# One core of a hybrid SSD and HGRN2 layer: HGRN's tile products grouped into seven visits, raised block by block

## The chip, the cores and the metric

The kernel runs on one core of one Trainium2 chip, and is written engine by engine: each engine's instructions stand in the order of the code and wait on semaphores. TensorE multiplies, VectorE, ScalarE and GpSimd work elementwise, SyncE issues most of the transfers. The metric is the device time of one execution in microseconds (us); lower is better.

## The reference

One inference step of a layer over 1,152 tokens (128 of context, 1,024 latent): a combined input projection feeds two mixers, a Mamba-2 SSD and an HGRN2, whose outputs are gated, merged and followed by a feed-forward block. What the change touches is HGRN2's scan, forward and backward, for each of 8 heads:

```python
c = HGRN_CHUNK
b = jnp.cumsum(log_f.astype(f32).reshape(bt, nc, c, n_heads, kd), axis=2)
causal = jnp.tril(jnp.ones((c, c), dtype=bool))[:, :, None, None]
decay = jnp.exp(jnp.where(causal, b[:, :, :, None] - b[:, :, None, :], -jnp.inf))
attn = jnp.einsum("bcihk,bcijhk,bcjhk->bcijh", qc, decay, kc)
o_intra = jnp.einsum("bcijh,bcjhv->bcihv", attn, vc)
contrib = jnp.einsum("bcjhk,bcjhv->bchkv", kc * jnp.exp(b[:, :, -1:] - b), vc)
...
o = o_f + o_b[:, ::-1]
```

The kernel takes chunks of 128 tokens. It builds `attn` of a chunk by levels: at level lv, blocks of 2^(lv-1) tokens meet their neighbours, with keys and queries that carry the decay up to the block's edge; between levels keys and queries are multiplied by the neighbour's decay ("raised").

## The kernel before

The token axis is cut into three blocks of 384 (`NB` = 3, `BW` = 384), a block into three chunks of 128 (`CB`). After a prologue the mixers run over 8 groups (`g`), one HGRN head and four SSD heads each. A group has two halves of 18 slots. In every slot TensorE projects one unit (a weight tile against one block): 24 matmuls of 384 columns into one of two banks that alternate, so that slot k needs the bank that slot k-2 filled to be free (`bank_free`). In the second half (`stage_b`) the slots 3 to 14 belong to convolution tiles; their unit is taken out of its bank in this order, in each slot k:

- ScalarE: `conv_tanh(k-1)`, which waits until VectorE has ended the taps of slot k-1; then `b_evac(k)`, a scaled copy of the bank to `acc`.
- VectorE: `conv_silu(k-1)` (th times acc, both in SBUF), which waits for that tanh; then `b_evac(k)`, four taps from the bank onto `acc`; the last one frees the bank. In slots 5, 8, 11 and 14 (block 0, context and latent) they are eight instructions. Once in three slots `low` subtracts a weight tile (`w_lo`).

Between these stands HGRN's work of the same group. TensorE makes the products of levels 0 to 7, three blocks each, 24 steps in all; a step is 12 matmuls of 32x32 tiles (levels 0 to 6) or 6 of 64x64 (level 7). Two steps follow the unit of each of the slots 0 to 11 (`steps_in`); such a stop between projection matmuls is called a visit here. Level lv from 1 to 5 needs a copy of the block's keys, ScalarE's `ka` (two buffers, `ka[i % 2]`, one of them a part of `kt_all`), levels 6 and 7 read `kq` itself. GpSimd raises a block with two multiplications of `kq` once TensorE has made its product (`lv_ready`), and tells by `up_ready`; ScalarE's copy for the next level waits for that. GpSimd walks the steps slot by slot too. VectorE collects a level's result when its third block is there (COPY_PREDICATED into `at_in`, one level a time; after level 5 four copies to `at_all`), and joins the decays of neighbouring blocks for the next levels (`join_decays`, at the slots of `JOINS`: 2, 4, 5, 6), in slots up to 4 ahead of silu and taps, in slots 5 and 6 behind them. The joins of slot 5 are two multiplications, those of slot 6 three. In slots 12 to 16 TensorE turns keys, sums states and makes the outputs. In the last group, g = 7, the second half has 24 units of gate columns instead; ScalarE alone empties their banks, and VectorE has no taps.

Nothing here is scheduled by a compiler: the order is the code's.

Of the kernel before, what the change touches and what calls it, by code (L numbers as in the profile page):

```python
# [540 lines left out]
def mixers(nc, scope, sb, sem, m):  # L541
# [75 lines left out]
    with ExitStack() as hgrn_scope:  # L617
# [82 lines left out]
    hrstd_ok, o_final, o_stored, soh_stored = sem("hrstd_ok"), sem("o_final"), sem("o_stored"), sem("soh_stored")  # L700

# [43 lines left out]
    with nc.Block() as block:  # L745
# [128 lines left out]
        def _(pe):  # L874
            def project(g, t, b, hb, cols_n=P):
# [120 lines left out]

            def hgrn(g, k):
                for i in steps_in(k):
                    lv, b = level(i)
                    if lv == 0:  # L1000
                        pe.wait_ge(q_ready, g * 3 + 1)
# [4 lines left out]
                    if b == 0:  # L1006
                        if lv == 1 or lv == 4:
                            pe.wait_ge(ms_read, g * NB + (2 if lv == 1 else 3))
                        elif lv == 3 or lv == 5:
                            pe.wait_ge(v_kept, g * NB + (2 if lv == 3 else 3))  # L1010
                        elif lv > IN_BLOCK:
                            pe.wait_ge(lv_merged.sem, lv_merged.at(g, 1 if lv == 6 else 5))
                    for j in range(CB):
                        c = b * CB + j
                        s = 1 << (lv - 1) if lv else 0
                        w = max(BS, s)
                        for t in range(P // w):
                            rows = slice(w * t, w * (t + 1))
                            out = lv_out(lv, b)[rows, j * w:(j + 1) * w]
                            own = slice(c * P + w * t, c * P + w * (t + 1))  # L1020
                            other = slice(c * P + w * (t ^ 1), c * P + w * ((t ^ 1) + 1))
                            if lv == 0:
                                last = pe.matmul(out, k_sum[:, own], q_t[:, own], start=True, stop=True)
                            elif lv <= IN_BLOCK:
                                last = pe.matmul(out.rearrange("p (n two s) -> p n two s", two=2, s=s),  # L1025
                                                 ka[i % 2][:, j * P + w * t:j * P + w * (t + 1)],
                                                 pairs(1, 2, s, c * P + w * t, w), start=True, stop=True)
# [122 lines left out]
            for k in range(8 * NB):  # L1150
                project(g, 6 + k // NB, k % NB, k % NB)
# [6 lines left out]
        def _(act):  # L1158
# [142 lines left out]

            def hgrn(g, k):
# [6 lines left out]
                for i in steps_in(k):  # L1309
                    lv, b = level(i)  # L1310
                    if lv == 0 or lv > IN_BLOCK:
                        continue
                    if lv == 1:
                        act.wait_ge(q_ready, g * 3 + 3)
                    else:
# [3 lines left out]
                    act.activation(ka[i % 2][:, :].rearrange("p (n two s) -> p n two s", two=2, s=s),  # L1319
                                   pairs(0, 3, s, b * BW, BW), ACT.Copy).then_inc(ka_ready.sem, 1)  # L1320
# [130 lines left out]
            def stage_b(g):  # L1451
                for k in range(SLOTS):
# [5 lines left out]
                    if k == 12:  # L1458
                        load_states(g)
# [1968 lines left out]
```

## Time and profile before

| | us |
|---|---|
| median of 3 runs | 3008.42 (3008.14 to 3009.68) |
| the profiled execution | 3008.66 |
| its span, first to last instruction | 3006.8 |
| TensorE busy in it | 2974.6 (99%) |
| VectorE, ScalarE, GpSimd busy | 1750.1, 1351.9, 941.0 |

The profiled execution lies 0.24 us over the median, and 1.9 us of it lie outside the span. The granted TensorE clock was 0.998 of full speed. A busy share of TensorE counts pipelined matmuls by modelled ends; how fast it goes is read from the distance between starts. Below, times inside the span are those of the group g = 2, whose second half begins at about 687 us; the other groups before g = 7 show the same pattern 202.25 us apart.

### The profile page before, as it was taken

What the parts mean: (1) busy time and instruction counts of PE and PEld (TensorE: products, weight loads), DVE (VectorE), ACT (ScalarE), POOL (GpSimd) and SP (SyncE); (2) the same over time, 40 slices, a digit from 0 to 9 for tenths busy, and PEclk for the clock granted to TensorE, in tenths of its full rate; (3) what the DMA queues carried; (4) which work ended last, traced back from release to release, by engine and by line L of the source; (5) the groups of instructions that cost most, each with busy time, mean ns of one, the idle gap of its engine ahead of it and who ended that gap; (6) DMA issues with size and microseconds to landing.
All of it is one profiled execution on the core that took longest, in us unless ns stands there. A gap on an engine that the chain in (4) does not pass through costs nothing. (4 is left out here: it accounts for less than half of the span.)

```text
span 3006.8 us, 57473 instructions
## 1 busy us (share of the span) xinstructions
PE 2974.6 (99%) x22229; PEld 2827.9 (94%) x22229; DVE 1750.1 (58%) x3007; ACT 1351.9 (45%) x2651; POOL 941.0 (31%) x1086
## 2 busy tenths in 40 slices
PE   7999999999999999999999999999999999999999
PEld 5899999999999999999999999999999999998887
DVE  4746857668577476585684624344378445555554
ACT  6445456455554554555645543211253222234443
POOL 0024435246245353462453430000113343340110
PEclk9999999999999999999999999999999999999999
DMA  7723122122122131221222325442312322227552
GB/s 266 260 69 102 49 79 81 48 78 81 47 89 73 59 99 43 83 81 49 74 80 67 118 80 161 141 124 86 122 40 61 87 65 76 76 65 248 201 184 103
DMA packets 294016, 300.29 MB, mean 100 GB/s; under 512 B 13240, under 2 KB 254768, under 8 KB 293808
## 3 DMA queue, kind: packets, MB, share of 16 engines
q1 hardware_dynamic: 247968, 230.17, 24.5%
q10 hardware_dynamic: 45840, 67.27, 7.1%
q8 instruction: 141, 2.31, 0.3%
q14 instruction: 67, 0.55, 0.1%
HBM read 247.93 MB, written 49.46 MB: 99 GB/s over the span
## 5 line engine op out<-in xcount | busy, mean ns | idle before, releaser
L889 PE MATMUL bank<-h_hi,w_hi 128*128 128x384 f32 x2496 | 863.4, 346 | 0.0
L889 PE MATMUL bank<-h_hi,w_lo 128*128 128x384 f32 x2496 | 835.7, 335 | 0.0
L889 PE MATMUL bank<-h_lo,w_hi 128*128 128x384 f32 x2496 | 834.9, 335 | 0.0
L889 PEld LDWEIGHTS bank<-h_hi,w_hi 128*128 128x128 f32 x2496 | 468.9, 188 | 12.7 <-issue 7.3
L889 PEld LDWEIGHTS bank<-h_lo,w_hi 128*128 128x128 f32 x2496 | 469.4, 188 | 0.6
L889 PEld LDWEIGHTS bank<-h_hi,w_lo 128*128 128x128 f32 x2496 | 468.6, 188 | 0.0
L2033 POOL TENSOR_TENSOR kq<-kq,fg 128x384 f32<-128x384 f32 x288 | 291.1, 1040 | 161.4 <-PE bank L1025 130.5
L1562 DVE SCALAR_TENSOR_TENSOR acc<-bank,taps,acc 128x372 f32<-128x372 f32 (+5 forms) x512 | 249.1, 507 | 68.0 <-ACT acc L1189 56.6
L1277 ACT ACTIVATE cumb<-cumb,tok_g 128x128 f32<-128x128 f32 x576 | 176.0, 389 | 75.5 <-POOL cumb L1994 75.5
L2440 PE MATMUL bank<-a_hi,v_hi 128*128 128x384 f32 x480 | 160.9, 335 | 2.9 <-DVEq L3238 1.9
L1530 DVE TENSOR_TENSOR w_lo<-raw,w_hi 128x1024 fp32r<-128x1024 f32 x104 | 140.4, 1350 | 38.3 <-ACT w_hi L1170 38.3
L2440 PE MATMUL bank<-a_hi,v_lo 128*128 128x384 f32 x480 | 160.4, 334 | 0.0
L2440 PE MATMUL bank<-a_lo,v_hi 128*128 128x384 f32 x480 | 160.4, 334 | 0.0
L2478 PE MATMUL bank<-a_hi,v_lo 128*128 128x288 f32 x480 | 141.6, 295 | 0.0
L2478 PE MATMUL bank<-a_hi,v_hi 128*128 128x288 f32 x480 | 141.2, 294 | 0.1
L2478 PE MATMUL bank<-a_lo,v_hi 128*128 128x288 f32 x480 | 141.3, 294 | 0.0
L1941 POOL TENSOR_TENSOR tok_g<-tok 128x36 f32<-128x36 f32 x16 | 4.2, 261 | 403.8 <-DVE q_t L1769 300.4
L1176 ACT ACTIVATE th<-acc 128x384 f32<-128x384 f32 x96 | 50.4, 525 | 173.6 <-DVE acc L1562 173.6
L1994 POOL TENSOR_SCALAR_AFFINE_SELECT cumb<-cumb 128x512 f32<-128x512 f32 x144 | 96.3, 691 | 83.5 <-DMA cumb<-cum_scratch 83.5
L1958 POOL TENSOR_TENSOR xp<-xb,tok_g 128x256 f32<-128x256 f32 x128 | 83.2, 657 | 114.5 <-PE bank L925 95.2
L3318 POOL MEMSET small<- 128x384 f32 x3 | 1.1, 418 | 373.7 <-issue 373.7
L2440 PE MATMUL bank<-b_hi,v_hi 128*128 128x384 f32 x336 | 113.0, 336 | 0.4 <-DVE b_lo L3225 0.2
(389 smaller groups left out, 6891.8 us busy)
## 6 DMA issues: line engine op xcount, KB each, us to landing
raw<-in_w_in SPq DMA_DIRECT2D x104, 512.0 KB, 4.0
raw<-in_ffn_w SPq DMA_DIRECT2D x78, 512.0 KB, 5.7
cumb<-cum_scratch SPq DMA_DIRECT2D x72, 512.0 KB, 6.1
ada_late<-in_ada_w SPq DMA_DIRECT2D x8, 2048.0 KB, 9.2
raw_d<-in_ffn_w SPq DMA_DIRECT2D x32, 512.0 KB, 5.3
small<-gate_scratch ACTq DMA_DIRECT2D x72, 192.0 KB, 2.4
hid_scratch<-small SPq DMA_DIRECT2D x20, 576.0 KB, 3.6
s_sum<-hid_scratch ACTq DMA_DIRECT2D x53, 192.0 KB, 3.6
```

The costliest lines, as they stand in the source:

```text
L889: last = pe.matmul(out, w[i][:, k, :], h[:, k, blk(hb)], start=(k == 0 and j == 0), stop=(k == KT - 1 and j == 2))
L1176: act.activation(th[ui][:, :], acc[ui][:, :], ACT.Tanh).then_inc(th_ok.sem, 1)
L1277: last = act.activation(e, e, ACT.Exp, bias=tok_g[:, 0, c, r:r + 1])
L1530: dve.tensor_tensor(w_lo[i][:, :, 0:width], raw[i][:, :, 0:width], w_hi[i][:, :, 0:width].bitcast(F32), ALU.subtract).then_inc(w_split.sem, 1)
L1562: ins = dve.scalar_tensor_tensor(out, src, taps[:, ti, j:j + 1], out, ALU.mult, ALU.add)
L1941: pool.tensor_tensor(dst[0], of_group(tok[:, 0, :, :], d), of_group(tok[:, 2, :, :], d), ALU.subtract)
L1958: return pool.tensor_tensor(out.rearrange("p (h c) -> p h c", c=HD), x.rearrange("p (h c) -> p h c", c=HD), w.rearrange("p (h a) -> p h a" ...
L1994: ins = pool.affine_select(v, v, [[0, HPG], [sign, P]], ALU.is_ge, far, base=0, channel_multiplier=-sign)
L2033: ins = pool.tensor_tensor(v, v, w.broadcast_to([P, 2, n, s]), ALU.mult)
L2440: last = pe.matmul(banks[3 * s + b][:, 0:BW], w[wp][:, k, :], operand[ap][:, k, blk(b)], start=(k == 0 and j == 0), stop=(k == kt - 1 and ...
L2478: last = pe.matmul(out, w[wi][:, k, :], mv, start=(o < 4 and k == 0 and i == 0), stop=(k == KH - 1 and i == 2), skip_group_check=o >= 4)
L3318: pool.memset(tmp[b][:, :], 0.0).then_inc(sums_zero, 1)
```

## The change

The two steps a slot are gone. A table `BURSTS` gives seven places, counted in eighths of a unit (three projection matmuls) from the half's start: levels 0 and 1 after slot 1's unit (16), level 2 in slot 3 (31), 3 in slot 5 (44), 4 in slot 7 (57), 5 in slot 8 (70), 6 in slot 10 (82), 7 in slot 11 (92); each place takes all three blocks. `project` stops inside a unit where the table says so. `ka` has a third buffer, a part of `hs_f`, so that each block has its own. GpSimd runs through `UPS`, all 21 raises, waiting for product, decay and the raise below, no longer slot by slot; level 7 goes in the order 0, 2, 1. ScalarE's copies stand in a table, most at a slot's start, two behind its tanh (`KA_LATE`). VectorE collects the levels in the slots of `MERGES`, and the joins of slot 5 move ahead of its silu and taps.

```diff
+BURSTS = {16: (0, 1), 31: (2,), 44: (3,), 57: (4,), 70: (5,), 82: (6,), 92: (7,)}
+KA_EARLY = {1: [(1, 0), (1, 1), (1, 2)], 2: [(2, 0)], 3: [(2, 1), (2, 2)], 4: [(3, 0), (3, 1)], 5: [(3, 2)],
+            6: [(4, 1), (4, 2)], 7: [(5, 0)], 8: [(5, 2)]}
+KA_LATE = {5: [(4, 0)], 7: [(5, 1)]}
+UPS = [(lv, b) for lv in range(1, LEVELS + 1) for b in ((0, 2, 1) if lv == LEVELS else range(NB))]
+MERGES = {2: (0, 1), 4: (2,), 5: (3,), 7: (4,), 9: (5,)}
+KEEPS = {10: [(6, 2)], 12: [(7, 1), (7, 2)]}
...
+        ka.append(hs_f[:, 3:6, :].rearrange("p c n -> p (c n)"))
...
+    up_ready = Count(sem("up_ready"), len(UPS))
...
+    def raised(eng, g, lv, b):
+
+        eng.wait_ge(up_ready.sem, up_ready.at(g, UPS.index((lv, b)) + 1))
...
-            def project(g, t, b, hb, cols_n=P):
+            def project(g, t, b, hb, cols_n=P, between=None):
...
                 for k in range(KT):
+                    if between is not None and k > 0:
+                        levels_at(g, KT * between + k)
                     for j, (w, h) in enumerate(((w_hi, h_hi), (w_hi, h_lo), (w_lo, h_hi))):
...
+            def levels_at(g, at):
+
+                for lv in BURSTS.get(at, ()):
+                    for b in range(NB):
+                        level_step(g, lv, b)
+
+            def level_step(g, lv, b):
+                i = step(lv, b)
+                if lv == 0:
+                    pe.wait_ge(q_ready, g * 3 + 1)
+                elif lv <= IN_BLOCK:
+                    pe.wait_ge(ka_ready.sem, ka_ready.at(g, i - NB + 1))
+                else:
+                    raised(pe, g, lv - 1, b)
+                if b == 0:
...
+                                             ka[b][:, j * P + w * t:j * P + w * (t + 1)],
...
             def hgrn(g, k):
-                for i in steps_in(k):
-                    lv, b = level(i)
...
-                    elif lv <= IN_BLOCK:
-                        pe.wait_ge(ka_ready.sem, ka_ready.at(g, i - NB + 1))
-                    else:
-                        pe.wait_ge(up_ready.sem, up_ready.at(g, i - 2 * NB + 1))
...
+                levels_at(g, KT * (k + 1))
                 for i in turns_in(k):
                     kind, b = TURNS[i]
                     if i == 0:
-                        pe.wait_ge(up_ready.sem, up_ready.at(g, LEVELS * NB))
+                        pe.wait_ge(lv_ready.sem, lv_ready.at(g, NSTEP))
+                    if i < 3:
+                        raised(pe, g, LEVELS, b)
...
-                    project(g, 6 + k // NB, k % NB, b_tile(k)[1])
+                    project(g, 6 + k // NB, k % NB, b_tile(k)[1], between=k)
...
+            def gather_keys(g, lv, b):
+
+                if lv == 1:
+                    act.wait_ge(q_ready, g * 3 + 3)
+                else:
+                    raised(act, g, lv - 1, b)
+                s = 1 << (lv - 1)
+                act.activation(ka[b][:, :].rearrange("p (n two s) -> p n two s", two=2, s=s),
+                               pairs(0, 3, s, b * BW, BW), ACT.Copy).then_inc(ka_ready.sem, 1)
+
+            def hgrn_late(g, k):
+                for lv, b in KA_LATE.get(k, ()):
+                    gather_keys(g, lv, b)
+
...
-                for i in steps_in(k):
-                    lv, b = level(i)
-                    if lv == 0 or lv > IN_BLOCK:
-                        continue
-                    if lv == 1:
-                        act.wait_ge(q_ready, g * 3 + 3)
-                    else:
-                        wait(up_ready, g, i - 2 * NB + 1)
-                    wait(lv_ready, g, i - 1)
-                    s = 1 << (lv - 1)
-                    act.activation(ka[i % 2][:, :].rearrange("p (n two s) -> p n two s", two=2, s=s),
...
+                for lv, b in KA_EARLY.get(k, ()):
+                    gather_keys(g, lv, b)
+                for lv, b in KEEPS.get(k, ()):
+                    wait(lv_ready, g, step(lv, b) + 1)
...
                     if k > 0 and (k - 1) // NB in CONV_TILES:
                         b_th_free(g, k - 1)
                         conv_tanh(g, k - 1)
+                    hgrn_late(g, k)
...
-                for i in steps_in(k - 1):
-                    lv, b = level(i)
-                    if lv > IN_BLOCK or b < NB - 1:
-                        continue
-                    wait(lv_ready, g, i + 1)
+                for lv in MERGES.get(k, ()):
+                    wait(lv_ready, g, step(lv, NB - 1) + 1)
...
-                if k in JOINS and k <= 4:
+                if k in JOINS and k <= 5:
...
-                    if k in JOINS and k > 4:
+                    if k in JOINS and k > 5:
...
-            def hgrn(g, k):
-                for i in steps_in(k):
-                    lv, b = level(i)
-                    if lv == 0:
-                        continue
+            def hgrn(g):
+                for lv, b in UPS:
+                    wait(lv_ready, g, step(lv, b) + 1)
+                    if lv == 1:
+                        pool.wait_ge(q_ready, g * 3 + 3)
+                    else:
+                        raised(pool, g, lv - 1, b)
+                    if lv in (2, 3, 4, 6):
+                        wait(decay_ok, g, {2: 1, 3: 2, 4: 3, 6: 4}[lv])
...
```

On TensorE, in group 0, around the product of level 2's last block and level 3's first, the kernel before has (bank4 and bank6 hold levels 3 and 2, `w_hi0`, `w_lo0` the weights of a projection):

```order
L889 MATMUL bank1<-h_hi,w_hi0 128x384
L889 MATMUL bank1<-h_lo,w_hi0 128x384
L889 MATMUL bank1<-h_hi,w_lo0 128x384
L1025 MATMUL bank6<-kq,ka 32x32 x12
L1025 MATMUL bank4<-kq,kt_all 32x32 x12
L889 MATMUL bank0<-h_hi,w_hi0 128x384
L889 MATMUL bank0<-h_lo,w_hi0 128x384
```

and the changed kernel, at level 3 in the middle of slot 5's unit:

```order
L899 MATMUL bank0<-h_hi,w_hi0 128x384
L899 MATMUL bank0<-h_lo,w_hi0 128x384
L899 MATMUL bank0<-h_hi,w_lo0 128x384
L1040 MATMUL bank4<-kq,ka 32x32 x12
L1040 MATMUL bank4<-kq,kt_all 32x32 x12
L1040 MATMUL bank4<-kq,hs_f 32x32 x12
L899 MATMUL bank0<-h_hi,w_hi0 128x384
L899 MATMUL bank0<-h_lo,w_hi0 128x384
```

Three steps stand together where two stood, and the unit goes on in the same bank behind them.

On VectorE, in slots 4 and 5 of group 0, from slot 4's join to the start of slot 6 (L1543 is silu, L1562 the taps, L1694 a join, L1720 a level collected), the kernel before has:

```order
L1694 TENSOR_TENSOR fg<-kt_all 128x2x288
L1530 TENSOR_TENSOR w_lo<-raw,w_hi 128x1024
L1543 SCALAR_TENSOR_TENSOR b_t<-th,acc 128x384
...
L1720 COPY_PREDICATED at_in<-masks,bank 128x288
L1543 SCALAR_TENSOR_TENSOR b_t<-th,acc 128x384
L1562 SCALAR_TENSOR_TENSOR acc<-bank,taps,acc 128x126
...
L1694 TENSOR_TENSOR fg<-fg 128x2x144
L1694 TENSOR_TENSOR fg<-fg 128x2x72
```

and the changed kernel (L1566 is silu, L1585 the taps, L1717 a join, L1740 a level collected):

```order
L1740 COPY_PREDICATED at_in<-masks,bank 128x288
L1717 TENSOR_TENSOR fg<-kt_all 128x2x288
L1553 TENSOR_TENSOR w_lo<-raw,w_hi 128x1024
L1566 SCALAR_TENSOR_TENSOR b_t<-th,acc 128x384
...
L1740 COPY_PREDICATED at_in<-masks,bank 128x288
L1717 TENSOR_TENSOR fg<-fg 128x2x144
L1717 TENSOR_TENSOR fg<-fg 128x2x72
L1566 SCALAR_TENSOR_TENSOR b_t<-th,acc 128x384
L1585 SCALAR_TENSOR_TENSOR acc<-bank,taps,acc 128x126
```

A level is collected ahead of slot 4's join, and the two joins of slot 5, which stood behind its taps, stand ahead of its silu.

## Rows read from the trace of the kernel before

**Rows 1.** The page's costliest groups: projection matmuls, count, busy, mean, idle before

```profile
L889 PE MATMUL bank<-h_hi,w_hi 128*128 128x384 f32 x2496 | 863.4, 346 | 0.0
```

**Rows 2.** Timeline (start, length, operation, count), TensorE, slot 4's visit

```profile
710.38 0.34 PE L889 MATMUL bank<-h_hi,w_lo 128*128 128x384 f32 x1
710.64 0.40 PE L1025 MATMUL bank<-kq,ka 128*32 128x32 f32 x24
710.86 0.42 PE L1025 MATMUL bank<-kq,kt_all 128*32 128x32 f32 x24
711.21 0.44 PE L889 MATMUL bank<-h_hi,w_hi 128*128 128x384 f32 x1
711.49 0.34 PE L889 MATMUL bank<-h_lo,w_hi 128*128 128x384 f32 x1
```

**Rows 3.** Timeline, TensorE, projection matmuls around the visits of slots 10 and 11

```profile
739.94 0.34 PE L889 MATMUL bank<-h_hi,w_lo 128*128 128x384 f32 x1
...
741.31 0.34 PE L889 MATMUL bank<-h_lo,w_hi 128*128 128x384 f32 x1
...
745.12 0.34 PE L889 MATMUL bank<-h_hi,w_lo 128*128 128x384 f32 x1
...
746.52 0.34 PE L889 MATMUL bank<-h_lo,w_hi 128*128 128x384 f32 x1
```

**Rows 4.** Timeline, GpSimd, levels 1 and 2 raised

```profile
696.51 3.57 POOL L2033 TENSOR_TENSOR kq<-kq,fg 128x384 f32<-128x384 f32 x2 [11.60 <-PE bank L1025]
701.27 4.64 POOL L2033 TENSOR_TENSOR kq<-kq,fg 128x384 f32<-128x384 f32 x4 [1.19 <-PE bank L1025]
706.23 4.53 POOL L2033 TENSOR_TENSOR kq<-kq,kt_all 128x384 f32<-128x384 f32 x4 [0.32 <-PE bank L1025]
711.16 2.87 POOL L2033 TENSOR_TENSOR kq<-kq,kt_all 128x384 f32<-128x384 f32 x2 [0.40 <-PE bank L1025]
```

**Rows 5.** Timeline, ScalarE, the key copy of level 2's second block

```profile
703.64 0.57 ACT L1319 ACTIVATE kt_all<-kq 128x384 f32<-128x384 f32 x1 [1.77 <-POOL kq L2033]
```

**Rows 6.** Timeline, VectorE, slots 4 and 5 and the joins of slot 5

```profile
709.80 2.04 DVE L1530 TENSOR_TENSOR w_lo<-raw,w_hi 128x1024 fp32r<-128x1024 f32 x1
...
713.06 2.53 DVE L1562 SCALAR_TENSOR_TENSOR acc<-bank,taps,acc 128x372 f32<-128x372 f32 x4
715.51 0.48 DVE L1720 COPY_PREDICATED at_in<-masks,bank 128x288 f32<-128x288 uint8 x1
716.18 1.24 DVE L1543 SCALAR_TENSOR_TENSOR b_t<-th,acc 128x384 f32<-128x384 f32 x1 [0.19 <-ACT th L1176]
717.34 3.03 DVE L1562 SCALAR_TENSOR_TENSOR acc<-bank,taps,acc 128x126 f32<-128x126 f32 x8
720.29 0.80 DVE L1694 TENSOR_TENSOR fg<-fg 128x288 f32<-128x288 f32 x2
```

**Rows 7.** Timeline, TensorE, first matmul of the units of slots 6 and 7

```profile
716.13 0.44 PE L889 MATMUL bank<-h_hi,w_hi 128*128 128x384 f32 x1
...
721.06 0.44 PE L889 MATMUL bank<-h_hi,w_hi 128*128 128x384 f32 x1
```

**Rows 8.** Timeline, VectorE, slot 7's weight tile; slot 8's silu

```profile
725.47 1.22 DVE L1530 TENSOR_TENSOR w_lo<-raw,w_hi 128x1024 fp32r<-128x1024 f32 x1
...
737.36 0.56 DVE L1543 SCALAR_TENSOR_TENSOR c_t<-th,acc 128x384 f32<-128x384 f32 x1
```

**Rows 9.** Timeline, VectorE, g = 7: the joins of slots 5 and 6

```profile
1723.78 2.33 DVE L1694 TENSOR_TENSOR fg<-fg 128x288 f32<-128x288 f32 x2
...
1728.94 1.15 DVE L1694 TENSOR_TENSOR fg<-fg 128x72 f32<-128x72 f32 x2
1730.12 0.82 DVE L1694 TENSOR_TENSOR hdec<-fg 128x18 f32<-128x18 f32 x1
```

**Rows 10.** Timeline, GpSimd, g = 7, beside them

```profile
1722.72 3.23 POOL L2033 TENSOR_TENSOR kq<-kq,kt_all 128x384 f32<-128x384 f32 x3
...
1728.24 3.55 POOL L2033 TENSOR_TENSOR kq<-kq,fg 128x384 f32<-128x384 f32 x4 [0.47 <-PE bank L1025]
```

More of the change, by code:

```diff
@@ L700, in mixers, with step @@
     hrstd_ok, o_final, o_stored, soh_stored = sem("hrstd_ok"), sem("o_final"), sem("o_stored"), sem("soh_stored")
+    def step(lv, b):
+        return lv * NB + b
+    def raised(eng, g, lv, b):
+        eng.wait_ge(up_ready.sem, up_ready.at(g, UPS.index((lv, b)) + 1))
     def parts_at(k):
@@ L994, in turn_v @@
                 last.then_inc(v_turned, 1)
-            def hgrn(g, k):
-                for i in steps_in(k):
-                    lv, b = level(i)
-                    if lv == 0:
-                        pe.wait_ge(q_ready, g * 3 + 1)
-                    elif lv <= IN_BLOCK:
-                        pe.wait_ge(ka_ready.sem, ka_ready.at(g, i - NB + 1))
-                    else:
-                        pe.wait_ge(up_ready.sem, up_ready.at(g, i - 2 * NB + 1))
[L1006 to L1027, printed above, removed]
-                            else:
-                                last = pe.matmul(out, (kf_t, kb_t)[t % 2][:, own], (qf_t, qb_t)[t % 2][:, other],
-                                                 start=True, stop=True)
-                    last.then_inc(lv_ready.sem, 1)
@@ new lines, in levels_at @@
+            def levels_at(g, at):
[11 more added lines that the diff above has]
+                if b == 0:
+                    if lv == 1 or lv == 4:
+                        pe.wait_ge(ms_read, g * NB + (2 if lv == 1 else 3))
+                    elif lv == 3 or lv == 5:
+                        pe.wait_ge(v_kept, g * NB + (2 if lv == 3 else 3))
+                    elif lv > IN_BLOCK:
+                        pe.wait_ge(lv_merged.sem, lv_merged.at(g, 1 if lv == 6 else 5))
+                for j in range(CB):
+                    c = b * CB + j
+                    s = 1 << (lv - 1) if lv else 0
+                    w = max(BS, s)
+                    for t in range(P // w):
+                        rows = slice(w * t, w * (t + 1))
+                        out = lv_out(lv, b)[rows, j * w:(j + 1) * w]
+                        own = slice(c * P + w * t, c * P + w * (t + 1))
+                        other = slice(c * P + w * (t ^ 1), c * P + w * ((t ^ 1) + 1))
+                        if lv == 0:
+                            last = pe.matmul(out, k_sum[:, own], q_t[:, own], start=True, stop=True)
+                        elif lv <= IN_BLOCK:
+                            last = pe.matmul(out.rearrange("p (n two s) -> p n two s", two=2, s=s),
+                                             ka[b][:, j * P + w * t:j * P + w * (t + 1)],
+                                             pairs(1, 2, s, c * P + w * t, w), start=True, stop=True)
+                        else:
+                            last = pe.matmul(out, (kf_t, kb_t)[t % 2][:, own], (qf_t, qb_t)[t % 2][:, other],
+                                             start=True, stop=True)
+                last.then_inc(lv_ready.sem, 1)
@@ L1150, in _ @@
             for k in range(8 * NB):
-                project(g, 6 + k // NB, k % NB, k % NB)
+                project(g, 6 + k // NB, k % NB, k % NB, between=k)
                 if k == 0:
@@ L1483, in _ @@
                 hgrn(g, k)
+                hgrn_late(g, k)
                 if k == SLOTS - 1:
@@ L1689, in join_decays @@
                 if k == 4:
-                    wait(up_ready, g, NB)
+                    raised(dve, g, 1, NB - 1)
                 for lv in range(lo, hi):
@@ L1703, in hgrn @@
             def hgrn(g, k):
-                for i in steps_in(k - 1):
-                    lv, b = level(i)
-                    if lv > IN_BLOCK or b < NB - 1:
-                        continue
-                    wait(lv_ready, g, i + 1)
+                for lv in MERGES.get(k, ()):
+                    wait(lv_ready, g, step(lv, NB - 1) + 1)
                     out = at_in[:, :].rearrange("p (c i) -> p c i", i=BS)
@@ L1895, in _ @@
                     split_squares(g)
-                if k in JOINS and k > 4:
+                if k in JOINS and k > 5:
                     join_decays(g, k)
@@ L2043, in _ @@
                     ssd(g, k)
-                for k in range(SLOTS):
-                    if k == 0:
-                        wait(silu_done, g, 0)
-                        gather_taps(g + 1)
-                    hgrn(g, k)
+                wait(silu_done, g, 0)
+                gather_taps(g + 1)
+                hgrn(g)
                 for k in early:
@@ L2053, in _ @@
                 ssd(g, k)
-            for k in range(SLOTS):
-                hgrn(g, k)
+            hgrn(g)
 PHASES = [("s1", 4), ("s2", 4), ("h", 4), ("o", 4), ("up0", 2)]
```

21 lines of the change are left out of this document (1 added, 20 removed).

## The prediction

> **What bounds the kernel now.** I read the page's engine shares first, then TensorE's list of waits, which names nothing in a second half, then the timelines of one second half. TensorE is busy in 2974.6 of 3006.8 us, and the projection matmuls, over a quarter of the span in their first form alone, never stand idle in front of one [rows 1]. So what TensorE does between them is paid in full, and whatever makes it wait is new. But the chain that frees its banks is nearly as slow. Slot 4's taps end at 713.06 + 2.53 = 715.59, and slot 6's unit, which writes into that bank, starts at 716.13; slot 5's end at 720.37, slot 7's unit starts at 721.06 [rows 6, 7]. The margins are 0.54 and 0.69 us. A slot lasts 721.06 - 716.13 = 4.93 us.
>
> **What a visit costs.** From the last projection matmul before slot 4's visit to the second one behind it are 711.49 - 710.38 = 1.11 us [rows 2]. Without a visit these are two distances between starts. A unit is 4.93 less the visit, over 24 matmuls: 0.174 each, so the visit costs 1.11 - 0.35 = 0.76, and a unit 4.17. The second step starts 0.22 us behind the first (710.86 and 710.64); from it to the next projection are 0.35. A step is then about 0.20 and the visit's fixed part 0.76 - 2 x 0.20 = 0.36 (0.32 by 0.22 a step, 0.40 by 0.18). A rule of the Trainium skill (TensorEngine Tiling (Array Packing), Tiling Modes) says that changing the tiling mode, not merely the tile, drains TensorE; the distances of 0.26 before the first small matmul and 0.28 behind the next projection, against 0.174, are in line with it.
>
> **What is saved on TensorE.** Twelve visits become seven: 5 x 0.36 = 1.8 us a group. Slot 10's visit, in which both tile sizes stand, costs 1.37 - 0.35 = 1.02, slot 11's 1.40 - 0.35 = 1.05 [rows 3]. By 0.36 + 0.20 + half of (1.05 - 0.36) slot 10's should be 0.91; the 0.1 over that goes too. That is 1.9 a group (1.7 to 2.1), 15 us in eight. All other matmuls stay. Of a visit with three steps the trace shows none: I take 0.36 + 3 x 0.20 = 0.96, between 0.92 and 1.03.
>
> **The new waits, slot by slot.** A second half's slot 2 starts about 19.7 us ahead of slot 6, at 696.4, in both kernels, since one visit of six steps (1.56) takes the place of two.
>
> Level 2, slot 3. Its visit comes 7/8 into the unit: 696.4 + 4.17 + 3.65 = 704.2; its third block is wanted at 704.7. Its keys are copied once GpSimd has raised level 1's third block. The six multiplications take 3.57 + 4.64 = 8.2 us back to back [rows 4], and the start can't be much before 696.5, since VectorE's weight tile is in work then as before: raised at 704.7, plus a copy of 0.57 [rows 5] and 0.1 of signals, 705.4. Wait 0.7 (0.4 if the start is 0.3 earlier, 1.0 if it is later).
>
> Slot 5's joins, the heart of it. Slots 4 to 6 now start at 706.4 (4.17 + 0.96 + 0.7 on), 710.6 and 715.7, and slot 7's unit wants its bank at 719.9. VectorE in slot 4 has a level to collect ahead (0.48), but its w_lo comes when GpSimd has ended level 2 (704.7 + 6.0) and waits for level 3's visit at 712.7; alone a w_lo takes 1.22 instead of 2.04 and a silu 0.56 instead of 1.24 [rows 6, 8]. So slot 4's taps end at about 715.5, as before: no wait for slot 6. Then, in slot 5, the joins stand ahead of the silu, while GpSimd raises level 3 (from 713). What two joins cost under a running GpSimd, g = 7 shows: 2.33 us instead of 0.80, and those of slot 6 1.15 + 0.82 [rows 6, 9, 10]. Each join, silu or w_lo seems to wait for GpSimd's multiplication in work to end, and GpSimd takes its next turn between two of them; the taps, which read a bank, show 2.53 in both slots. The Trainium skill (GPSIMD Engine Reference, Key points) states this the same way: GpSimd shares its SBUF interfaces with VectorE, and contends with instructions of two SBUF inputs. By it too this change puts the joins where they are dearest; without the rule the row stands. Slot 5's run is 0.48 + 2.33 + 1.24 + 3.03 = 7.08 less 0.2 of overlaps, from 715.5 to 722.4. Wait 2.5 us in front of slot 7's unit (0.3 if joins and silu cost 0.80 and 0.56; 3.0 at most, from the margin in slot 4). All VectorE and ScalarE work behind is queued on it, and GpSimd idles: level 4's visit lies in slot 7.
>
> Slots 6 to 12. Slot 7 starts at 722.4, slot 8 at 727.6, slot 9 wants its bank at 732.7. Slot 6's taps follow a tanh of 0.5, a silu of 0.56 and end at 726.1, in time. Behind them come slot 6's three joins under a running GpSimd (2.0 by g = 7, up to 3.0 if all three wait), a level collected 0.48, w_lo 1.22, silu 0.56, taps 2.53: 726.1 + 6.8 to 7.8 = 732.9 to 733.9. Wait 0.2 to 1.2; I take 1.0, since level 4 is in full work. Before, GpSimd happened to pause there. Levels 5 to 7 add 0.5 for slots 10 to 12 (level 5's collection with its four copies ahead of slot 9's silu), bounds 0 and 1.5.
>
> Slots 12 to 17 keep their work and its order; nothing in them gives a delay back, since the unit that comes late is TensorE's own and the next group starts behind it. SyncE's loads wait for weight tiles that come in step with the slots; the third key buffer lies in `hs_f` rows written only from slot 14 on: nothing.
>
> **The sum.** A group g = 0 to 6: -1.9 + 0.7 + 2.5 + 1.0 + 0.5 = +2.8 us; seven give +19.6. In g = 7 VectorE frees no bank: there remain the 1.9 gained and waits for keys. Joins and collection lie beside level 1 to 3 there, at two to three multiplications' delay, 1.1 us (0 to 1.9): -0.8. Together +18.8, on the profiled execution's 3008.66 us 3027.5; the median lies 0.24 lower: **3027 us**. The terms won't all fall to one side; half of their spreads gives +1.4 to +3.6 a group, 3017 to 3034 us.
>
> **The rivals.** (a) *The banks come in time.* If VectorE's instructions fall into GpSimd's pauses, as the joins of slots 5 and 6 do before, no bank is late: 7 x (-1.9 + 0.7) - 0.8 = -9, about 2999 us; without the wait for keys 2993. For it: no bank is late today, and what GpSimd's phase is worth is 0.7 us in one silu and 1.5 in two joins. Against it: GpSimd has no slot to wait for any more, so it runs longer in one piece. (b) *Only half of it.* The joins of slot 5 slip through, the later waits stay: -1.9 + 0.7 + 0.4 + 0.5 + 0.4, about +0.1 a group: 3008. (c) *GpSimd falls behind too.* Between the visits of levels 6 and 7 are 10 eighths and a visit, 5.2 + 0.96 = 6.2 us, for six multiplications of 0.89 (3.55 for four, rows 10) plus what VectorE takes from them, 5.3 to 6.6. If each of the last three levels is late by 0.4, add 1.2 a group: 3036. It decides from the point where a level takes longer than its visits are apart. (d) *A visit's price is all in its steps*, so that fewer visits save nothing: then 3027 + 15 = 3042; against it, 0.26 and 0.28 stand at slot 4's ends where 0.174 is the pace, and 0.35 behind the start of its last step where 0.22 lie between its two.
>
> **Chances.** The forecast 0.60, (a) 0.17, (b) 0.13, (c) 0.08, (d) 0.02. Faster by over 0.2% (6 us, about what a measurement of this kernel can tell from no change) is (a) and a little of (b): 0.18. Within 0.2%: 0.12. Slower: 0.70. The range from 2999 to 3035 takes in the forecast, (b), half of (a) and half of (c).
>
> **What would show it.** In the profile after: L899 with idle time in front, released by VectorE's taps, mostly at slot 7; the two joins of slot 5 with over 2 us together where they took 0.80; a start of slot 12 some 2.8 us later against the group's start, not 1.9 earlier; a visit of three steps at 0.96; GpSimd idle for over 3 us ahead of level 4. Wrong would be the case if slot 5's joins stay near 0.8 us, if a three-step visit costs clearly more than 1.0, or if the groups before g = 7 get shorter.

## The result, and the profile after

| | before | after |
|---|---|---|
| median (range), us | 3008.28 (3007.45 to 3009.68), 4 runs | 3025.39 (3024.33 to 3028.7), 4 runs |
| the profiled execution, span | 3008.66, 3006.8 | 3028.7, 3026.9 |
| seven distances from group to group, g = 0 to g = 7 | 1416.7 | 1432.8 |
| g = 7, from its pair of matmuls (below) to the end of slot 13's turns | 76.4 | 75.4 |

The ratio is 1.0058 (95% interval 1.0046 to 1.0069): slower by 17.1 us, where 19 were forecast. Every median and ratio here and in the experiments is of executions at a mean granted clock of 0.99 and more; one of the ten of experiment e8 ran at 0.654 (4184.6 us) and is left out of its median.

The distances between groups come from one short pair of TensorE matmuls that stands once in each. The view of a line's instructions gives their first and last start; the first row is before's, the second after's (the last start is that of the pair's second matmul, 0.2 us behind its first):

```profile
L977 PE MATMUL bank<-mm_r,ones_r x16: 338/338/339, 275.5 to 1692.4; 128*128 128x384 f32 x16
```

```profile
L987 PE MATMUL bank<-mm_r,ones_r x16: 338/338/339, 277.0 to 1710.0; 128*128 128x384 f32 x16
```

So 16.1 us are lost in the seven groups, and 1.0 is gained in g = 7. Before, six of the seven distances are 202.25 to 202.30 and one, from g = 2 to g = 3, is 203.07; 0.8 of that is a wait behind the second half that stands in no other group and not in the profile after:

```profile
PE bank L947 <- DVE t_off L1609: 0.7, 1, 0.7
```

Against seven equal groups the loss is 16.9. The other 4.9 us by which the profiled execution is longer (20.0 less 16.1 - 1.0) are not the change's: 1.5 lie before the first group, and 3.3 are three waits in a stage behind the last one (L2490), which the profiles of some other kernels below show too and some don't. Behind the groups nothing else differs by more than 0.3.

The rows of the page's costliest groups that answer [rows 1], and GpSimd's and the weight tile's, with the idle time in front and what ended most of it:

```profile
L899 PE MATMUL bank<-h_hi,w_hi 128*128 128x384 f32 x2496 | 864.7, 346 | 14.4 <-DVE acc L1585 13.3
...
L2048 POOL TENSOR_TENSOR kq<-kq,fg 128x384 f32<-128x384 f32 x288 | 284.1, 1021 | 186.7 <-PE bank L1040 164.6
...
L1553 DVE TENSOR_TENSOR w_lo<-raw,w_hi 128x1024 fp32r<-128x1024 f32 x104 | 146.9, 1412 | 36.0 <-ACT w_hi L1190 35.9
```

The projection matmuls, which never stood idle, now stand idle for 14.4 us, and 13.3 of it ended with VectorE's taps. TensorE's list of waits (us in total, times, longest) says how often:

```profile
PE bank L899 <- DVE acc L1585: 13.3, 7, 1.9
```

Seven times, once in each group but the last. The timelines of g = 2 show the place. VectorE (slots 4 and 5, in answer to [rows 6]), GpSimd, and TensorE around slot 7's first matmul:

```profile
716.87 2.06 DVE L1553 TENSOR_TENSOR w_lo<-raw,w_hi 128x1024 fp32r<-128x1024 f32 x1
718.85 0.55 DVE L1566 SCALAR_TENSOR_TENSOR b_t<-th,acc 128x384 f32<-128x384 f32 x1
...
721.76 0.48 DVE L1740 COPY_PREDICATED at_in<-masks,bank 128x288 f32<-128x288 uint8 x1
722.12 1.97 DVE L1717 TENSOR_TENSOR fg<-fg 128x288 f32<-128x288 f32 x2
724.02 1.27 DVE L1566 SCALAR_TENSOR_TENSOR b_t<-th,acc 128x384 f32<-128x384 f32 x1
725.21 3.03 DVE L1585 SCALAR_TENSOR_TENSOR acc<-bank,taps,acc 128x126 f32<-128x126 f32 x8
```

```profile
711.34 6.51 POOL L2048 TENSOR_TENSOR kq<-kq,kt_all 128x384 f32<-128x384 f32 x6 [0.51 <-PE bank L1040]
719.29 5.58 POOL L2048 TENSOR_TENSOR kq<-kq,fg 128x384 f32<-128x384 f32 x6 [1.44 <-PE bank L1040]
730.12 3.38 POOL L2048 TENSOR_TENSOR kq<-kq,fg 128x384 f32<-128x384 f32 x4 [5.25 <-PE bank L1040]
```

```profile
726.06 0.34 PE L899 MATMUL bank<-h_hi,w_lo 128*128 128x384 f32 x1
728.29 0.59 PE L899 MATMUL bank<-h_hi,w_hi 128*128 128x384 f32 x1 [1.90 <-DVE acc L1585]
728.69 0.52 PE L899 MATMUL bank<-h_lo,w_hi 128*128 128x384 f32 x1
729.01 0.52 PE L899 MATMUL bank<-h_hi,w_lo 128*128 128x384 f32 x1
729.46 0.55 PE L1040 MATMUL bank<-kq,ka 128*32 128x32 f32 x24
```

The two joins run from 722.12 to 724.09 beside GpSimd's level 3 (719.29 to 724.87), and the silu, to 725.28, starts beside its last multiplication. Joins and silu take 1.97 and 1.27 us; the joins alone took 0.80 [rows 6]. The taps end at 728.24, and slot 7's unit starts at 728.29, 2.23 behind the matmul before it, where 0.174 is the pace: a wait of 2.06.

The last rows show something that the forecast has nothing of: behind the wait the matmuls start 0.32 apart (728.69, 729.01), not 0.174. The view of stretches (length, busy time of PE, PEld, DVE, ACT, POOL, then the granted clock, DMA share, GB/s), 3.2 us behind the wait of groups 2 and 3:

```profile
728.50:731.70 3.20, 3.20 (x78) 2.70 (x78) 2.70 (x5) 1.86 (x3) 1.58 (x2) 0.50 0.02 5
933.60:936.80 3.20, 3.20 (x86) 2.91 (x86) 2.71 (x5) 2.29 (x4) 2.19 (x3) 1.00 0.02 5
```

In groups 1, 2, 4 and 5 the clock falls to 0.50 (1.2 of 2.4 GHz) for 3.4 us behind the wait, in groups 0, 3 and 6 it does not, though all seven waits are 2.00 to 2.09 us long. The distance to the next group is 205.05 to 205.09 in the four, 204.15 to 204.17 in the three, and was 202.26 before: 4 x 2.8 + 3 x 1.9 is the 16.9. The lower clock costs 0.9 us a group, net of small waits that then disappear.

Where the 1.9 us of a group without it come from, by the distances of the matmuls of g = 6: the seven visits cost 8.43 us against 9.87 for twelve, -1.44; slot 7's wait of 2.08 and the 0.11 by which the second matmul behind a stop comes late, +2.19; and small waits for a bank ahead of slots 6, 9, 10 and 11 of 0.27, 0.11, 0.32 and 0.36, +1.06. The sum is +1.8; the distances give 1.87.

### The profile page after: what moved, and what is told of

It reads as the page before. It is cut to its first block and busy times, and to the rows that moved or that the text cites. A ratio compares the mean times of both kernels' runs of the same rounds, so it can differ in the third digit from the quotient of the medians.

```text
span 3026.9 us, 57369 instructions
## 1 busy us (share of the span) xinstructions
PE 2976.3 (98%) x22229; PEld 2830.2 (94%) x22229; DVE 1766.0 (58%) x3007; ACT 1354.5 (45%) x2651; POOL 927.5 (31%) x1086
## 5 line engine op out<-in xcount | busy, mean ns | idle before, releaser
L899 PE MATMUL bank<-h_hi,w_hi 128*128 128x384 f32 x2496 | 864.7, 346 | 14.4 <-DVE acc L1585 13.3
L2048 POOL TENSOR_TENSOR kq<-kq,fg 128x384 f32<-128x384 f32 x288 | 284.1, 1021 | 186.7 <-PE bank L1040 164.6
L1585 DVE SCALAR_TENSOR_TENSOR acc<-bank,taps,acc 128x372 f32<-128x372 f32 (+5 forms) x512 | 249.1, 507 | 67.8 <-ACT acc L1209 57.3
L1553 DVE TENSOR_TENSOR w_lo<-raw,w_hi 128x1024 fp32r<-128x1024 f32 x104 | 146.9, 1412 | 36.0 <-ACT w_hi L1190 35.9
L2490 PE MATMUL bank<-a_hi,v_hi 128*128 128x288 f32 x480 | 141.3, 294 | 1.9 <-DVE small L3081 1.0
L2490 PE MATMUL bank<-a_hi,v_lo 128*128 128x288 f32 x480 | 141.6, 295 | 0.0
L2490 PE MATMUL bank<-a_lo,v_hi 128*128 128x288 f32 x480 | 141.3, 294 | 0.0
```

What stands on the lines that cost most here:

```text
L899: last = pe.matmul(out, w[i][:, k, :], h[:, k, blk(hb)], start=(k == 0 and j == 0), stop=(k == KT - 1 and j == 2))
L1553: dve.tensor_tensor(w_lo[i][:, :, 0:width], raw[i][:, :, 0:width], w_hi[i][:, :, 0:width].bitcast(F32), ALU.subtract).then_inc(w_split.sem, 1)
L1585: ins = dve.scalar_tensor_tensor(out, src, taps[:, ti, j:j + 1], out, ALU.mult, ALU.add)
L2048: ins = pool.tensor_tensor(v, v, w.broadcast_to([P, 2, n, s]), ALU.mult)
L2490: last = pe.matmul(out, w[wi][:, k, :], mv, start=(o < 4 and k == 0 and i == 0), stop=(k == KH - 1 and i == 2), skip_group_check=o >= 4)
```

## The experiments

The ratio of each run is to executions of the kernel before that were measured together with it; "seven groups" is the distance of the rows above, 1416.7 before (1415.9 without the single wait) and 1432.8 after. What the expectations call the period is the distance from one group to the next.

| run | median, us | ratio to before (95%) | seven groups |
|---|---|---|---|
| e1, slot 5's joins behind its taps | 3008.56 | 0.9998 (0.9989 to 1.0008) | 1416.1 |
| e2, GpSimd holds for the joins | 3012.88 | 1.0014 (1.0004 to 1.0024) | 1422.2 |
| e3, before, joins ahead of the silu | 3011.06 | 1.0006 (0.9996 to 1.0015) | 1419.7 |
| e4, visit 4 in the wait | 3013.21 | 1.0016 (1.0006 to 1.0025) | 1422.1 |
| e5, four more visits | 3025.96 | 1.0060 (1.0043 to 1.0076) | 1434.0 |
| e6, joins twice | 3029.98 | 1.0069 (1.0053 to 1.0086) | 1442.9 |
| e7, five joins on GpSimd | 3003.88 | 0.9985 (0.9976 to 0.9995) | 1414.0 |
| e8, before, five joins on GpSimd | 3007.56 | 0.9996 (0.9986 to 1.0006) | 1415.8 |
| e9, slot 4's join there too | 3003.65 | 0.9982 (0.9973 to 0.9991) | 1413.0 |
| e10, and visit 4 in slot 7's front | 3001.91 | 0.9979 (0.9970 to 0.9988) | 1411.4 |

**e1: is it the joins' place?**

```diff
-                if k in JOINS and k <= 5:
+                if k in JOINS and k <= 4:
...
-                    if k in JOINS and k > 5:
+                    if k in JOINS and k > 4:
```

> The changed kernel with slot 5's two joins put back behind its taps, all else as changed. Theory (the 2.06 us that TensorE waits in front of slot 7's unit come from the joins that stand ahead of the silu and meet GpSimd's multiplications): the silu starts about 1.9 us sooner, the wait falls below 0.5 us, the half-clock stretch of 3.4 us behind it is gone in all groups, the two joins, now behind GpSimd's level 3, take 0.8 us together; about 3010 us (3006 to 3014). Rival (GpSimd in one piece makes VectorE late wherever the joins stand): the wait stays over 1.5 us, over 3018 us.

VectorE in slot 5, and the end of slot 6's unit with the start of slot 7's:

```profile
716.09 0.84 DVE L1566 SCALAR_TENSOR_TENSOR b_t<-th,acc 128x384 f32<-128x384 f32 x1 [0.20 <-ACT th L1196]
717.07 3.04 DVE L1585 SCALAR_TENSOR_TENSOR acc<-bank,taps,acc 128x126 f32<-128x126 f32 x8
720.03 0.79 DVE L1717 TENSOR_TENSOR fg<-fg 128x288 f32<-128x288 f32 x2
```

```profile
719.72 0.34 PE L899 MATMUL bank<-h_hi,w_lo 128*128 128x384 f32 x1
720.17 0.44 PE L899 MATMUL bank<-h_hi,w_hi 128*128 128x384 f32 x1
```

The wait fell from 2.06 to 0.28, the joins cost 0.79, and no group has a stretch at the lower clock. All of the loss is gone, by this one edit. But no gain is left either: the visits still cost 1.46 us less a group, and waits of 0.27, 0.39, 0.08, 0.32 and 0.34 ahead of slots 6, 7, 9, 10 and 11 (each with the late second matmul behind it) take 1.4 of it back.

**e2: the place, or GpSimd beside it?**

```diff
-                        wait(decay_ok, g, {2: 1, 3: 2, 4: 3, 6: 4}[lv])
+                        wait(decay_ok, g, 3 if (lv, b) == (3, 1) else {2: 1, 3: 2, 4: 3, 6: 4}[lv])
```

> The changed kernel; GpSimd waits with block 1 of level 3 until slot 5's two joins are done, so that these run alone at the same place. Theory (contention, not the place, makes up most of it): the joins take 0.45 + 0.3 us instead of 1.02 + 0.91, the wait in front of slot 7's unit falls from 2.06 to about 0.9 (silu still against a multiplication), about 3014 us (3009 to 3018). Rival (the place alone costs, whatever GpSimd does): joins under 0.8 us and the wait still about 2 us, or joins at 1.9 us as they were; 3025 us.

VectorE and GpSimd around the joins:

```profile
717.87 0.79 DVE L1717 TENSOR_TENSOR fg<-fg 128x288 f32<-128x288 f32 x2
718.58 0.55 DVE L1566 SCALAR_TENSOR_TENSOR b_t<-th,acc 128x384 f32<-128x384 f32 x1
```

```profile
714.96 1.83 POOL L2048 TENSOR_TENSOR kq<-kq,fg 128x384 f32<-128x384 f32 x2 [1.37 <-PE bank L1040]
718.83 3.71 POOL L2048 TENSOR_TENSOR kq<-kq,fg 128x384 f32<-128x384 f32 x4 [2.04 <-DVE fg L1717]
```

The same two joins in the same place, without a multiplication beside them, take 0.79 instead of 1.97, and the silu, which GpSimd no longer meets either, 0.55 instead of 1.27. That is 1.9 us, and slot 7's wait falls from 2.06 to 0.25: at this place it was contention nearly in full, more than expected. But the loss has moved. GpSimd, held up, starts level 4 in time for slot 6's silu, and slot 9's unit now waits:

```profile
723.54 1.23 DVE L1566 SCALAR_TENSOR_TENSOR b_t<-th,acc 128x384 f32<-128x384 f32 x1 [1.35 <-ACT th L1196]
```

```profile
723.48 5.46 POOL L2048 TENSOR_TENSOR kq<-kq,fg 128x384 f32<-128x384 f32 x6 [0.94 <-PE bank L1040]
```

```profile
732.49 0.34 PE L899 MATMUL bank<-h_hi,w_lo 128*128 128x384 f32 x1
733.54 0.41 PE L899 MATMUL bank<-h_hi,w_hi 128*128 128x384 f32 x1 [0.71 <-DVE acc L1585]
```

That is 1.05 from start to start, a wait of 0.87.

The Trainium skill (SBUF — State Buffer, Terms) calls the port pair of VectorE and GpSimd an exclusive lock, held for a whole instruction. The runs agree: the joins, of 0.45 and 0.31 us alone (e2), take 1.02 and 0.91 beside multiplications of about 0.93. In the changed kernel's g = 2 the first ends at 723.15, 0.32 behind the end of the multiplication that it met, the second at 724.09, 0.17 behind the end of the next.

**e3: the moved joins alone, in the kernel before.** The edit is e1's, turned round: `k <= 4` becomes `k <= 5` and `k > 4` becomes `k > 5`.

> The kernel before with one part of the change alone: slot 5's two joins ahead of its silu instead of behind its taps. GpSimd raises there too, in shorter pieces. Theory: the second join and the silu meet a multiplication, the taps end 1.1 to 1.9 us later against a margin of 0.69, a wait of 0.4 to 1.2 us in front of slot 7's unit in every group, 3014 us (3010 to 3017). Rival (only GpSimd's long run of the changed kernel makes joins dear): 0.8 us for both, a wait of at most 0.1, 3008 to 3009 us.

```profile
716.00 1.39 DVE L1694 TENSOR_TENSOR fg<-fg 128x288 f32<-128x288 f32 x2
717.31 1.27 DVE L1543 SCALAR_TENSOR_TENSOR b_t<-th,acc 128x384 f32<-128x384 f32 x1
```

The first join starts in a pause of GpSimd's and takes its 0.45; only the second is held up by a multiplication (0.91). Slot 7's unit is late by 0.4 us in every group, the low end of what was expected. The median's interval includes 1, so the loss is read from the groups: 202.72 to 202.79 apart in six of seven, against 202.25 to 202.30. One part of the change gives a loss by itself. That it grows to 2.06 us takes the other parts too: both joins meet a multiplication (1.97 instead of 1.39), and the 0.69 that slot 7 had to spare is gone before they start, for e1, without them, already waits 0.28.

**e4: fill the wait.**

```diff
-BURSTS = {16: (0, 1), 31: (2,), 44: (3,), 57: (4,), 70: (5,), 82: (6,), 92: (7,)}
+BURSTS = {16: (0, 1), 31: (2,), 44: (3,), 56: (4,), 70: (5,), 82: (6,), 92: (7,)}
```

> The changed kernel with level 4's visit one eighth earlier: ahead of slot 7's first projection matmul, which waits 2.06 us for its bank, instead of one eighth behind it. Its keys are there at about 725.5 in the profiled second half, the visit would start at 726.1. Theory (a wait of TensorE is paid in full and can be filled): the visit's 0.99 us a group are hidden, and since TensorE then stands still for 1.1 us only, the stretches at half clock get fewer; GpSimd starts level 4 about 3 us sooner and meets slot 6's silu, which may give back up to 0.7 us a group at slot 9: 3016 us (3012 to 3020). Rival (all of it is given back at slot 9 by VectorE, which is the bound there): 3025 us.

```profile
721.91 0.40 PE L1040 MATMUL bank<-kq,ka 128*32 128x32 f32 x24
...
723.82 0.44 PE L899 MATMUL bank<-h_hi,w_hi 128*128 128x384 f32 x1 [1.05 <-DVE acc L1585]
```

The visit now stands in the wait, of which 1.05 us are left idle (1.15 in g = 0, the most); the lower clock is gone from all groups. The gain is 12.2 us, more than the 9 expected. Of it 10.7 lie in the seven groups: seven hidden visits are 6.9, four stretches at the lower clock 3.6. GpSimd's earlier start gave back 0.1 us a group, at slot 10, not 0.7.

**e5: what is a visit's fixed price?** Levels 5 and 6 are visited one block at a time:

```diff
-BURSTS = {16: (0, 1), 31: (2,), 44: (3,), 57: (4,), 70: (5,), 82: (6,), 92: (7,)}
+BURSTS = {16: (0, 1), 31: (2,), 44: (3,), 57: (4,), 70: ((5, 0),), 71: ((5, 1),), 72: ((5, 2),), 82: ((6, 0),), 83: ((6, 1),), 84: ((6, 2),), 92: (7,)}
...
-                    for b in range(NB):
-                        level_step(g, lv, b)
+                    for one, b in [lv] if isinstance(lv, tuple) else [(lv, b) for b in range(NB)]:
+                        level_step(g, one, b)
```

> The changed kernel with the visits of levels 5 and 6 taken apart again, one block a visit, one eighth of a unit between them: four more visits a group, the same 24 steps. Theory (a visit has a fixed price of about 0.36 us beside 0.2 a step): a visit of one step costs 0.5 to 0.6 us in the trace, four more cost 1.4 us a group, 11.5 in eight groups, of which the waits of 0.3 to 0.4 at slots 9 and 12 may swallow up to 0.7 a group: 3033 us (3030 to 3038). Rival (the price is all in the steps): 0.33 a visit, 3025 us.

```profile
736.78 0.34 PE L899 MATMUL bank<-h_hi,w_lo 128*128 128x384 f32 x1
737.05 0.40 PE L1040 MATMUL bank<-kq,kt_all 128*32 128x32 f32 x24
737.38 0.45 PE L899 MATMUL bank<-h_hi,w_hi 128*128 128x384 f32 x1
737.66 0.34 PE L899 MATMUL bank<-h_lo,w_hi 128*128 128x384 f32 x1
```

The same visit in one piece, in the changed kernel (g = 3, projection matmuls only):

```profile
941.59 0.34 PE L899 MATMUL bank<-h_hi,w_lo 128*128 128x384 f32 x1
...
942.64 0.45 PE L899 MATMUL bank<-h_hi,w_hi 128*128 128x384 f32 x1
942.92 0.34 PE L899 MATMUL bank<-h_lo,w_hi 128*128 128x384 f32 x1
```

A visit of one step costs 737.66 - 736.78 - 0.35 = 0.53, the late matmul behind it included; three cost 1.59 where one of three steps costs 942.92 - 941.59 - 0.35 = 0.98 (0.99 before rounding). The two visits more are 0.6, so the fixed price is 0.30 us and a step 0.23. The time, though, is 3026 and not 3033: the expectation missed. The four visits add 1.2 us a group, yet the commonest distance of two groups without the lower clock is 204.53 against 204.16, 0.4 more. The other 0.8 filled the waits of slots 9 to 11 (0.11, 0.32 and 0.36), which are gone, and only one group of seven has a stretch at the lower clock instead of four, behind waits of the same length (2.00 to 2.11). Where VectorE sets the pace, TensorE's work counts for little in either direction: 1.2 us added cost 0.4, and in e1 1.46 saved brought nothing.

**e6: double the suspect.** `join_decays` runs its list of levels twice for slot 5.

> The changed kernel with slot 5's two joins run twice in the same place. Theory (each waits for the multiplication that GpSimd has in work, and GpSimd ends level 3 at about 724.9 in the profiled second half): the third join still meets it, the fourth and the silu run alone (0.31 and 0.56 us), so that the wait in front of slot 7's unit grows from 2.06 by about 0.9 only, to 2.9 us; the 3.4 us at half clock follow in all seven groups instead of four; 3031 us (3028 to 3035). Rival (two joins cost 1.93 us there whatever GpSimd has left to do): wait 4.0 us, 3038 us.

```profile
722.91 3.40 DVE L1718 TENSOR_TENSOR fg<-fg 128x288 f32<-128x288 f32 x4
726.23 0.55 DVE L1566 SCALAR_TENSOR_TENSOR b_t<-th,acc 128x384 f32<-128x384 f32 x1
```

```profile
729.79 0.44 PE L899 MATMUL bank<-h_hi,w_hi 128*128 128x384 f32 x1 [2.60 <-DVE acc L1585]
```

Four joins take 3.40, and the silu behind them, GpSimd being done, 0.55 instead of 1.27: the wait grows by 0.7 to 2.77, not by 1.9. The price hangs on what GpSimd still has to do. The lower clock follows in six of seven groups, twice for 6.8 us; the median, 3030, is near the 3031 expected.

**e7 and e8: relieve VectorE, with and without the change.** GpSimd runs the joins of slots 5 and 6 itself, between levels 3 and 4; VectorE's calls for `k > 4` are dropped (in e8 the same, ahead of block 0 of level 4):

```diff
+            def join_on_pool(g):
+
+                for lv in range(3, 8):
+                    if lv > 3:
+                        pool.wait_ge(pool_step, g * 3 + {4: 1, 5: 1, 6: 2, 7: 3}[lv])
+                    if lv == 5:
+                        wait(decay_ok, g, 3)
+                    ins = pool.tensor_tensor(decays[lv], decays[lv - 1][:, :, 0::2], decays[lv - 1][:, :, 1::2],
+                                             ALU.mult)
+                    ins.then_inc(decay_ok.sem if lv in (4, 7) else pool_step, 1)
...
                 for lv, b in UPS:
+                    if (lv, b) == (4, 0):
+                        join_on_pool(g)
```

> The changed kernel with all five joins of slots 5 and 6 taken from VectorE and run on GpSimd between levels 3 and 4, where it is idle for 5.2 us. Theory (what eats the 1.43 us that the merged visits save a group is VectorE, late at slots 7 and 9 by 0.36 and 0.37 us in the run with the joins behind the taps, period 202.31): both waits go, the period falls to 201.6 or less, GpSimd takes 1.5 to 2.5 us for the five; 3003 us (2999 to 3006). Rival (the joins on GpSimd hold VectorE's silu and w_lo up as much as they relieve it): period 202.2 to 202.6, 3008 to 3011 us.

> The kernel before with the same five joins on GpSimd between levels 3 and 4, its twelve visits unchanged. Theory (without merged visits TensorE waits for nothing, so relief of VectorE is worth nothing): period 202.26 as before, 3008 to 3009 us. Rival (VectorE's relief pays by itself, and the visits have no part in it): as much faster as the changed kernel gets by it, 3003 us. A loss is possible where GpSimd's raise of level 4 starts up to 2 us later and a step of TensorE waits for it: up to 3015 us.

GpSimd in e7, in a stretch where it was idle:

```profile
1122.58 1.95 POOL L2035 TENSOR_TENSOR fg<-fg 128x288 f32<-128x288 f32 x4
1124.61 0.22 POOL L2035 TENSOR_TENSOR hdec<-fg 128x18 f32<-128x18 f32 x1
1125.44 3.39 POOL L2057 TENSOR_TENSOR kq<-kq,fg 128x384 f32<-128x384 f32 x4 [0.61 <-PE bank L1040]
```

The five joins take 2.3 us there, and level 4 starts behind them only when its product is there. Two groups of e7 are 201.88 apart in most cases (202.31 in e1, 202.26 before), though not 201.6: slot 10's wait is gone, those of slots 6, 7 and 11 stay, at 0.27, 0.39 and 0.34 in e1's measure. (The second wait that the expectation puts at slot 9 stands at slot 10 in e1's profile; slot 9 has 0.08.) In the kernel before the same relief leaves 202.25: without merged visits TensorE waited for nothing. So the merged visits pay, by 0.4 us a group, only together with less work on VectorE.

**e9 and e10: what is left.** In e9 slot 4's join goes to GpSimd as well, ahead of level 3; e10 is e9 with e4's table.

> The kernel with five joins on GpSimd, and slot 4's join (level 2's factors) there too, ahead of level 3, where GpSimd is idle for 1.5 us (1115.55 to 1117.02 in its profile). VectorE's slot 4 loses 0.75 us. Theory (what is left of TensorE's waits is VectorE again, 0.31 us at slot 6 behind slot 4's taps and 0.25 at slot 7): the wait at slot 6 goes, slot 7's goes with it in part; period 201.4 to 201.6 us instead of 201.88, 3001 us (2999 to 3004). Rival (GpSimd needs 1.0 to 1.3 us for this join, so level 3 starts later and its multiplications meet slot 5's silu and slot 6's work): period 201.8 to 202.3, 3003 to 3007 us.

> The same, and level 4's visit ahead of slot 7's first projection matmul instead of one eighth behind it. Theory (a visit fills a wait at its place and costs nothing where there is none): period lower by what is left of slot 7's wait, 0 to 0.25 us, so 3000 to 3002 us. Rival (with GpSimd's five joins in between, level 4's keys are there too late for the earlier visit, or its earlier raise meets slot 6's silu): period higher by 0.1 to 0.6 us, up to 3007 us.

```profile
1114.30 1.46 POOL L2035 TENSOR_TENSOR fg<-kt_all 128x576 f32<-128x576 f32 x1
1115.93 5.64 POOL L2057 TENSOR_TENSOR kq<-kq,fg 128x384 f32<-128x384 f32 x6 [0.17 <-POOL fg L2035]
```

The join (1.46 us) fits ahead of level 3, and slot 6's wait is gone. But the distance falls to 201.83 only, not to the 201.4 to 201.6 expected: slot 10's unit is late again, by 0.33; TensorE, no longer late at slot 6 and less at slot 7, asks for that bank sooner, and slot 8's silu takes 1.26 instead of 1.11. Level 3 also starts later and holds up slot 5's silu (1.23 instead of 0.83), as the rival had it. e10 takes what was left at slot 7: 201.63. It is the fastest of all, 3001.9 us, 0.2% under the kernel before. The intervals of e7, e9 and e10 overlap; the distances between groups order them.

## Why the prediction was right, step by step

**The sum.** 3027 against 3025.4. The groups lost 16.1 us where 19.6 were forecast, g = 7 gained 1.0 against 0.8. The heart of it, the joins under a running GpSimd, is shown by e1, e2 and e6: put behind the taps, or left alone in their place, they leave 0.28 and 0.25 of slot 7's wait of 2.06; run twice they add 0.7. The terms, a group:

| term | forecast | measured (g = 6) |
|---|---|---|
| visits, with the waits for keys in them | -1.9 + 0.7 = -1.2 | -1.44 |
| slot 6's bank | 0 | +0.27 |
| slot 7's bank | +2.5 | +2.19 |
| slot 9's bank | +1.0 | +0.11 |
| slots 10 to 12 | +0.5 | +0.68 |
| lower clock, in four groups of seven | none | +0.9 |
| together | +2.8 | +1.8 (1.9 by the distances), with the lower clock +2.8 |

**Visits.** Right in kind: one of three steps costs 0.99 (0.96 forecast). The split was a little off: the fixed price is 0.30 and not 0.36, a step 0.23 and not 0.20 (e5), so that five visits fewer are worth 1.5 us and not 1.8. Rival (d) is out. The first two visits took 1.81 and 1.22 for six and three steps: the second waited 0.23 for its keys and not 0.7, the first 0.1 to 0.25, by the measured or the forecast price of its steps. Less these waits the visits save 1.8 to 1.9, as forecast.

**Slot 6.** Wrong by a little: slot 4's w_lo was taken at 1.22, because GpSimd should have ended level 2. It had not (711.34 + 6.51 = 717.85), and w_lo took 2.06 as before.

**Slot 7.** Mechanism right, size near: the joins took 1.97 and not the 2.33 of g = 7, where GpSimd's multiplications are longer: 3.23 for three [rows 10] against 5.58 for six.

**Slot 9.** The term that was mis-sized most. The forecast had TensorE's lateness in it: slot 9 was to want its bank 10.3 us behind slot 7's start, and in g = 6 it did at 10.4; slot 6's taps were to end 3.7 behind that start, and did. What was too dear is the run from there: 7.6 us were taken (a wait of 1.0), 6.6 came, below the 6.8 of the cheapest case. Slot 6's three joins took 1.9 and not the 2.8 implied, for the first was hardly held up (0.27 us); the w_lo took 1.59 instead of 1.22, and 0.4 of overlaps, which the sum had not taken off here, gave that back. In g = 2 the joins did take 2.4 us, but there the lower clock delays TensorE's demand as well. In the groups without that clock 0.11 is left.

**The clock.** No term stood for it. That the total came near is partly luck: 0.9 us in four groups (3.6 us) stand against a slot 9 charged 0.9 too high in seven (6.2 us). Slot 6 (+0.27) and slot 7 (-0.3) nearly cancel.

**The rivals.** (a), banks in time, came out only with the joins moved (e1), and gave 3008, not 2999: the saved time is lost again in waits of 0.3 us, for VectorE's chain was within 0.7 us of TensorE's. (b), only half of the waits, did not come: the joins never slipped between the multiplications. (c) did not come: GpSimd stood idle 5.25 us ahead of level 4, and levels 5 to 7 kept their places.

**Left open.** Why four of seven equal waits are followed by the lower clock and three are not, and why in e5 only one of seven is; and 1 to 2 us of the median's 17.1, which neither the groups (16.1 or 16.9) nor g = 7 account for.

## What to carry to other kernels

Before saving time on the engine that is 99% busy, measure how much the chain that feeds it has to spare: here 0.5 to 0.7 us a slot, and a saving of 1.4 us a group came back as waits of 0.3 to 0.4 at four slots, until the chain was relieved too. An instruction with two SBUF inputs on VectorE pays, beside its own time, for the rest of the multiplication that GpSimd has in work (0.31 us became 0.91); put it where GpSimd pauses, or give it to GpSimd in that pause. If TensorE must wait at a known place, put work of its own there: in e4 that hid the visit, and with 1.05 to 1.15 us of the wait left no group's clock fell.

## What the runs showed of the hardware

The granted clock of TensorE went to 0.50 for 3.4 us around or behind single waits inside the loop, with the engine at full work before and after: in none of the 28 groups of e1 to e4 (g = 0 to 6), whose longest wait was 1.15 us (e4), in 4 of 7 after waits of 2.00 to 2.09, in only 1 of 7 after the same waits in e5, and in 6 of 7 with waits of 2.7 to 2.8 (e6), two of them for 6.8 us. Behind the groups every one of the twelve profiles has one more wait of this size (1.9 us idle, at L2440 before, which the profile puts down to VectorE's queue), and the clock fell behind it in three, e1, e4 and e9. The stretch behind that wait, before and in e1:

```profile
1823.20:1826.40 3.20, 3.20 (x20) 3.20 (x19) 0.00 (x0) 1.06 (x1) 0.00 (x0) 1.00 0.96 280
1821.50:1824.70 3.20, 3.20 (x12) 3.20 (x11) 0.00 (x0) 1.06 (x1) 0.00 (x0) 0.50 0.95 266
```

In such a stretch projection matmuls start 0.32 us apart instead of 0.174, and a three-step visit with the two distances beside it takes 2.0 to 2.1 us instead of 1.34. Where the clock falls, a wait of 2 us is thus worth 3.

Each stop of TensorE costs 0.1 us more than its length: the second matmul behind it starts 0.25 to 0.28 behind the first, not 0.174, as it does behind a visit.
